# A two-layer diffusion step on one core: more of the merge in units of seven products, retention values centred beforehand, slot transposes reordered

## What is computed

```python
def _retention_output(o, g, gain):
    mu = jnp.mean(o, axis=-1, keepdims=True)
    var = jnp.mean(jnp.square(o - mu), axis=-1, keepdims=True)
    on = ((o - mu) * lax.rsqrt(var + EPS)).reshape(b, n, C_V).astype(g.dtype) * gain
    return jax.nn.silu(g) * on

def _merge(gates, a_o, b_o, c_o, w_pa, w_pb, w_pc, w_o):
    br = jnp.stack([a_o @ w_pa, b_o @ w_pb, c_o @ w_pc], axis=2)   # 3 x [tokens, 1024]
    merged = jnp.sum(jax.nn.sigmoid(gates) * br, axis=2)           # gates: 3 x [tokens, 1024]
    return merged @ w_o
```

## Time and profile before

| what | value |
|---|---|
| median of 3 runs | 1939.27 us (1939.24 to 1939.88) |
| profiled execution | 1939.07 us, of which its span is 1937.2 us |
| TensorE busy | 1818.0 us, 94% of the span |
| DVE, ACT, POOL busy | 638.3, 360.1, 210.0 us |
| moved by DMA | 553.10 MB, 286 GB/s over the span |
| mean granted TensorE clock | 0.999 of full speed |

### The profile page before, as it was taken

How to read it: one execution, slowest core, us unless ns; L and a number is a source line. 1 busy time by engine, 2 the same in 40 slices (tenths; PEclk the granted TensorE clock), 3 DMA queues, 4 the chain that set the end, 5 groups by cost and what they waited for, 6 DMA issues and landing times.

```text
span 1937.2 us, 21171 instructions
## 1 busy us (share of the span) xinstructions
PE 1818.0 (94%) x8802; PEld 1001.0 (52%) x8802; DVE 638.3 (33%) x1268; ACT 360.1 (19%) x835; POOL 210.0 (11%) x115
## 2 busy tenths in 40 slices
PE   6999999999999988788799999999999999888887
PEld 3565566799544433233365555669975343333323
DVE  2633347564211211111155333665532112111113
ACT  3223331111211110010132242221012010101002
POOL 0200003551100000000002000136400000000000
PEclk9999999999999999999999999999999999999999
DMA  9515151335799999999992244214456999999996
GB/s 391 200 72 223 66 224 69 131 131 205 302 396 427 427 428 427 427 428 428 413 381 98 87 180 174 98 44 174 174 228 275 428 426 428 428 427 428 427 428 273
DMA packets 54847, 553.10 MB, mean 286 GB/s; under 512 B 5985, under 2 KB 9953, under 8 KB 13281
## 3 DMA queue, kind: packets, MB, share of 16 engines
q1 hardware_dynamic: 50976, 549.13, 68.5%
q10 hardware_dynamic: 3776, 2.62, 0.4%
HBM read 547.54 MB, written 4.19 MB: 285 GB/s over the span
## 4 chain that ended last, share of the span: by engine, by line
PE 70%; DMA 29%; ACT 0%; DVE 0%; issue 0%; SPq 0%; DVEq 0%; ACTq 0%
PE psum L1423 14%; PE psum L1020 12%; PE psum L1234 11%; DMA ring<-in_w_up 8%; DMA dense<-in_w_down 8%; DMA ring<-in_w_gate 8%; PE psum L1022 6%; PE psum L1316 4%; PE psum L1148 4%; DMA dense<-in_w_gate 4%; PE psum L447 2%; PE psum L982 2%; PE psum L1226 2%; PE psum L1068 1%; PE psum L1393 1%; PE psum L1002 1%
## 5 line engine op out<-in xcount | busy, mean ns | idle before, releaser
L1423 PE MATMUL psum<-ring,dense 128*64 128x512 f32 x960 | 216.3, 595 | 31.9 <-DMA ring<-in_w_gate 18.0
L1020 PE MATMUL psum<-hT,ring 128*128 128x384 f32 x720 | 238.8, 488 | 0.0
L1020 PEld LDWEIGHTS psum<-hT,ring 128*128 128x128 f32 x720 | 135.0, 190 | 90.7 <-issue 1.4
L1423 PE MATMUL psum<-dense 128*64 128x512 f32 x704 | 158.7, 595 | 23.7 <-DMA dense<-in_w_gate 16.8
L1423 PEld LDWEIGHTS psum<-ring,dense 128*64 128x64 f32 x960 | 68.6, 137 | 170.7 <-issue 139.6
L2181 DVE TENSOR_TENSOR state<-state,psum 128x512 f32<-128x512 f32 x32 | 22.0, 687 | 372.3 <-PE psum L1423 334.2
L1022 PE MATMUL psum<-ring,hT 128*128 128x512 f32 x288 | 126.5, 594 | 0.0
L1423 PEld LDWEIGHTS psum<-dense 128*64 128x64 f32 x704 | 49.2, 137 | 129.1 <-issue 94.8
L2218 DVE COPY decays<-psum 16x512 f32<-16x512 f32 x60 | 41.3, 689 | 220.6 <-PE psum L1423 220.2
L1835 ACT ACTIVATE kcT<-psum 32x512 f32<-32x512 f32 x60 | 35.3, 588 | 423.6 <-PE psum L1423 423.2
L812 POOL TENSOR_TENSOR tmp<-square 128x384 f32<-128x384 f32 x5 | 5.0, 996 | 873.0 <-ACT square L1543 873.0
(11 more groups left out here) (285 smaller groups left out, 2401.5 us busy)
## 6 DMA issues: line engine op xcount, KB each, us to landing
dense<-in_w_gate SPq DMA_DIRECT2D x34, 2048.0 KB, 35.7
ring<-in_w_in SPq DMA_DIRECT2D x60, 1024.0 KB, 9.7
ring<-in_w_up SPq DMA_DIRECT2D x30, 2048.0 KB, 37.6
ring<-in_w_gate SPq DMA_DIRECT2D x30, 2048.0 KB, 36.1
wide<-in_w_up SPq DMA_DIRECT2D x22, 2048.0 KB, 37.6
dense<-in_w_down SPq DMA_DIRECT2D x20, 2048.0 KB, 40.3
ring<-in_w_mod SPq DMA_DIRECT2D x38, 1024.0 KB, 9.0
ring<-in_w_down SPq DMA_DIRECT2D x18, 2048.0 KB, 40.1
```

What stands on the lines that cost most here:

```text
L1020: last = M.matmul(psum[:, bank, 0:T], ring[:, n % RING, k, cols], hT[:, k, :], start=k == 0, stop=k == KD - 1)
L1423: last = M.matmul(psum[HALF * half:HALF * (half + 1), bank, :], lhsT(k), SPARE_BLOCKS[2 * kk + half] if spare else w[:, kk, half * SLAB:(h ...
```

## The change

1. The last four chunks of the first branch become two more units: `ALONE = 4` chunks alone, `PAIRS = 10` units (unit u uses branch (u + 2) // 4 and gate slab 10 + u // 2). POOL makes the sums for them: gate slab 10, the tokens of the first branch, half of its weights.
2. The buffers of the sums are placed anew. They now reach into the place of expert buffer 0 until the last unit, so SP loads expert 0's first half after the chain slabs, when all units are done; ring places come free at other counts.
3. The values and states of the retention are centred by DVE (`center`: a sum and a combination, four times a layer). `c_mean`, its wait and its correction go. ACT squares each head straight from the bank. `c_out(3)` and `c_var(2)` stand ahead of the units, `c_var(3)` inside the first.
4. In the first layer `mod` of the third chain slab goes ahead of the first `modT`; one `modT` goes behind the slot transposes, another behind the first gather. The rows of the third slab go to another buffer.

The diff, cut to its core:

```diff
@@ -61,7 +61,8 @@
-PAIRS = KD
+ALONE = 4
+PAIRS = (3 * KD - ALONE) // 2
@@ -238,12 +239,14 @@
-SUMS_X = [dense[:, 5648 + n * 1024:6672 + n * 1024] for n in range(3)]
-SUMS_Y = [dense[:, 4608:5632], decay_cols, dense[:, 10768:11792]]
-SUMS_Z = [dense[:, 9744:10768], dense[:, 11792:12816], dense[:, 12816:13840]]
-GATE_SUMS = {11: SUMS_X, 12: SUMS_Z, 13: SUMS_X, 14: SUMS_Z}
+SUMS_X = [dense[:, 4608 + n * 1024:5632 + n * 1024] for n in range(3)]
+SUMS_Z = [dense[:, a:a + 1024] for a in (7680, 10752, 11776)]
+SUMS_Y = [dense[:, a:a + 1024] for a in (8704, 9728, 12800)]
+GATE_SUMS = {10: SUMS_X, 11: SUMS_Z, 12: SUMS_X, 13: SUMS_Z, 14: SUMS_X}
+FIRST_BRANCH_SUMS = [in_chunks(x, 2) for x in (decay_cols[:, 512:1024], wide_cols[:, 6144:6656], wide_cols[:, 7680:8192])]
-Z_SUMS = {1: [in_chunks(x, 2) for x in (act[:, 0:T], flat(state1)[:, 0:T], rs[:])],
+Z_SUMS = {0: [in_chunks(x, 2) for x in (rs[:], merged[:, 5, :], merged[:, 7, :])],
+          1: [in_chunks(x, 2) for x in (act[:, 0:T], flat(state1)[:, 0:T], decay_cols[:, 0:T])],
@@ -377,17 +380,16 @@
-cmean_full = sem("cmean_full", 4)
-ccen = sem("ccen", 4)
+centered = sem("centered", 4)
-gate_full = sem("gate_full", KD)
-gate_exp = sem("gate_exp", KD)
-br_full = sem("br_full", KD)
-combined = sem("combined", 36)
+gate_full = sem("gate_full", ALONE)
+gate_exp = sem("gate_exp", ALONE)
+br_full = sem("br_full", ALONE)
+combined = sem("combined", 48)
@@ -496,7 +498,7 @@
-return steps + [("mod",) + m[2], ("modT",) + m[1], ("modT",) + m[2]]
+return steps[0:2] + [("mod",) + m[2], ("modT",) + m[0], ("modT",) + m[1], ("modT",) + m[2]]
@@ -516,13 +518,14 @@
-EARLY_CHAIN = [5, 4]
+EARLY_CHAIN = [4, 4]
-SECOND_SUMS = {("gate", 0): 7, ("gate", 2): 20, ("gate", 4): 28, ("branch", 4): 30, ("gate", 6): 34}
-THIRD_SUMS = {("gate", 0): 16, ("branch", 4): 31, ("gate", 6): 35}
-LAST_SUMS = {("branch", 4): 32, ("gate", 6): 36}
+SECOND_SUMS = {("gate", 0): 7, ("branch", 0): 14, ("gate", 2): 20, ("branch", 2): 28, ("gate", 4): 32, ("gate", 6): 40,
+               ("branch", 6): 42, ("gate", 8): 46}
+THIRD_SUMS = {("gate", 0): 15, ("branch", 0): 16, ("branch", 6): 43, ("gate", 8): 47}
+LAST_SUMS = {("branch", 6): 44, ("gate", 8): 48}
@@ -530,7 +533,7 @@
-return xgT[:, u * SLAB:(u + 1) * SLAB]
+return act if u == CHAIN_MODS - 1 else xgT[:, u * SLAB:(u + 1) * SLAB]
@@ -641,14 +644,12 @@
-elif kind == "w_in" and j < 11:
-    eng.wait_ge(gate_full, at(gate_full, 4 * (j - 8)))
+elif kind == "w_in" and j == 9:
+    eng.wait_ge(gate_full, at(gate_full, ALONE))
-    eng.wait_ge(pair_full["gate"], at(pair_full["gate"], 14 * (j - 10)))
-elif kind == "branch" and j == 0:
-    eng.wait_ge(br_full, at(br_full, KD))
+    eng.wait_ge(pair_full["gate"], at(pair_full["gate"], 14 * (j - 9)))
-    eng.wait_ge(pair_full["branch"], at(pair_full["branch"], 28 * j))
+    eng.wait_ge(pair_full["branch"], at(pair_full["branch"], 28 * j + 14))
@@ -716,9 +717,9 @@
-    if i == 0:
-        sp.wait_ge(pair_full["gate"], at(pair_full["gate"], 42))
-    if i == 1:
+    if i == 2:
+        sp.wait_ge(pair_full["branch"], at(pair_full["branch"], 14))
+    else:
         sp.wait_ge(pair_full["gate"], at(pair_full["gate"], 7 * PAIRS))
         sp.wait_ge(pair_full["branch"], at(pair_full["branch"], 7 * PAIRS))
 elif i == 4:
@@ -758,13 +759,12 @@
-buffer_free(0)
-load_expert(0)
 for c, (l, j) in enumerate(CHAIN[layer]):
     buffer_free(CHAIN_AT[c])
     sp.dma_start(whole_slab(BUFFERS[layer][CHAIN_AT[c]]), w_mod[l, j]).then_inc(chain_in[c], 16)
-buffer_free(1)
-load_expert(1)
+for i in range(2):
+    buffer_free(i)
+    load_expert(i)
 load_spare()
@@ -862,6 +862,9 @@
+if b == 0:
+    weight_sums(lambda kh, nh: branch_quarter(layer, 0, kh, nh)[:, :, 1, :], FIRST_BRANCH_SUMS)
+    return
@@ -882,29 +885,35 @@
-pool.wait_ge(att_full, at(att_full, HEADS_C))
+pool.wait_ge(ko_st, at(ko_st, 32))
+gate_sums(10)
+pool.wait_ge(a_done, at(a_done, HEADS_A))
+pool.wait_ge(o_read, at(o_read, 8))
+first_sums(lambda th, kh: z_quarter(0, th, kh), Z_SUMS[0])
 pool.wait_ge(qd_ready, at(qd_ready, 4))
-pool.wait_ge(ko_st, at(ko_st, 32))
+branch_sums(0)
+pool.wait_ge(gate_full, at(gate_full, ALONE))
+last_sum(h_quarter)
+pool.wait_ge(br_full, at(br_full, ALONE))
+last_sum(lambda th, kh: z_quarter(0, th, kh))
+pool.wait_ge(co_full, at(co_full, HEADS_C))
+pool.wait_ge(c_done, at(c_done, HEADS_C))
+pool.wait_ge(v_stored, at(v_stored, 32))
 gate_sums(11)
-pool.wait_ge(o_read, at(o_read, 8))
-pool.wait_ge(co_full, at(co_full, HEADS_C))
+pool.wait_ge(att_ready, at(att_ready, HEADS_C))
 first_sums(lambda th, kh: z_quarter(1, th, kh), Z_SUMS[1])
 last_sum(lambda th, kh: z_quarter(1, th, kh))
-pool.wait_ge(att_ready, at(att_ready, HEADS_C))
-pool.wait_ge(c_done, at(c_done, HEADS_C))
-pool.wait_ge(v_stored, at(v_stored, 32))
 branch_sums(1)
-pool.wait_ge(gate_full, at(gate_full, KD))
-last_sum(h_quarter)
+pool.wait_ge(pair_full["gate"], at(pair_full["gate"], 14))
 gate_sums(12)
-pool.wait_ge(br_full, at(br_full, KD))
+pool.wait_ge(pair_full["branch"], at(pair_full["branch"], 14))
 first_sums(lambda th, kh: z_quarter(2, th, kh), Z_SUMS[2])
 last_sum(lambda th, kh: z_quarter(2, th, kh))
-pool.wait_ge(pair_full["gate"], at(pair_full["gate"], 14))
+pool.wait_ge(pair_full["gate"], at(pair_full["gate"], 28))
 gate_sums(13)
-pool.wait_ge(pair_full["branch"], at(pair_full["branch"], 28))
+pool.wait_ge(pair_full["branch"], at(pair_full["branch"], 42))
 branch_sums(2)
-pool.wait_ge(pair_full["gate"], at(pair_full["gate"], 28))
+pool.wait_ge(pair_full["gate"], at(pair_full["gate"], 42))
 gate_sums(14)
@@ -986,7 +995,8 @@
-pe.wait_ge(z_read, max(f_of("mod", l, j) + 1, f - 1))
+same_bank = filler_bank(f) == filler_bank(f - 1)
+pe.wait_ge(z_read, max(f_of("mod", l, j) + 1, f if same_bank else f - 1))
@@ -1153,6 +1163,8 @@
+if kind == 2:
+    pe.wait_ge(centered, at(centered, 3))
@@ -1177,6 +1189,7 @@
+pe.wait_ge(centered, at(centered, 4))
@@ -1190,14 +1203,6 @@
-def c_mean(h):
-    if h == 0:
-        pe.wait_ge(st_ev, at(st_ev, 1))
-    pe.wait_ge(co_read, at(co_read, h + 1))
-    if h >= 1:
-        pe.wait_ge(ccen, at(ccen, h))
-    M.matmul(psum[:, TR[0], 0:T], ones, c_raw[:, h % 2, :], start=True, stop=True).then_inc(cmean_full, 1)
@@ -1206,15 +1211,12 @@
-for m in range(KD):
-    if m < HEADS_C:
-        c_att(m)
-    if 1 <= m <= HEADS_C:
+for m in range(ALONE):
+    c_att(m)
+    if m >= 1:
-    if 2 <= m <= HEADS_C + 1:
-        c_mean(m - 2)
-    if 3 <= m <= HEADS_C + 2:
-        c_var(m - 3)
+    if m >= 2:
+        c_var(m - 2)
@@ -1238,15 +1240,15 @@
-return lambda k: x[:, k, u % 4 // 2, u % 2 * P:(u % 2 + 1) * P]
+return lambda k: x[:, k, (u + 2) % 4 // 2, u % 2 * P:(u % 2 + 1) * P]
-branch = 1 + u // 4
+branch = (u + 2) // 4
-    j = 11 + u // 2
+    j = 10 + u // 2
@@ -1254,9 +1256,12 @@
-sums = [branch_weights(x.rearrange("p (k h n) -> p k h n", k=2, h=2), u) for x in SUMS_Y]
+if branch:
+    sums = [branch_weights(x.rearrange("p (k h n) -> p k h n", k=2, h=2), u) for x in SUMS_Y]
+else:
+    sums = [gate_weights(x, u) for x in FIRST_BRANCH_SUMS]
-if u % 4 == 0:
+if u % 4 == 2:
@@ -1266,6 +1271,8 @@
+if kind == "gate" and u == 0:
+    c_var(HEADS_C - 1)
@@ -1273,9 +1280,11 @@
-elif kind == "branch":
-    pe.wait_ge(gate_exp, at(gate_exp, KD))
-    pe.wait_ge(br_read, at(br_read, KD))
+elif kind == "gate":
+    pe.wait_ge(co_read, at(co_read, HEADS_C))
+else:
+    pe.wait_ge(gate_exp, at(gate_exp, ALONE))
+    pe.wait_ge(br_read, at(br_read, ALONE))
@@ -1285,6 +1294,8 @@
+c_out(HEADS_C - 1)
+c_var(HEADS_C - 2)
@@ -1372,7 +1383,7 @@
-fill(CHAIN_FILL[layer][EARLY_CHAIN[layer]:])
+fill(CHAIN_FILL[layer][EARLY_CHAIN[layer]:EARLY_CHAIN[layer] + 1])
@@ -1499,6 +1510,7 @@
+fill(CHAIN_FILL[layer][EARLY_CHAIN[layer] + 1:])
@@ -1730,33 +1742,35 @@
-for m in range(KD):
...
+def inverse_norm(h):
+    sc.wait_ge(cvar_full, at(cvar_full, h + 1))
...
+def head_read(h):
+    sc.wait_ge(co_full, at(co_full, h + 1))
+    if h >= 2:
+        sc.wait_ge(cvar_full, at(cvar_full, h - 1))
+    A_.activation(square[:, h % 2, :], psum[:, O[h % 2], 0:T], ACT.Square).then_inc(csq, 1)
+    if h >= 2:
+        sc.wait_ge(c_done, at(c_done, h - 1))
+    A_.activation(c_raw[:, h % 2, :], psum[:, O[h % 2], 0:T], ACT.Copy).then_inc(co_read, 1)
+for m in range(ALONE):
+    if m >= 2:
+        inverse_norm(m - 2)
+    if m >= 1:
+        head_read(m - 1)
-sc.wait_ge(gate_exp, at(gate_exp, KD))
-A_.preload_act_table(ACT.Sigmoid)
@@ -1764,8 +1778,14 @@
+head_read(HEADS_C - 1)
+inverse_norm(HEADS_C - 2)
 for u in range(PAIRS):
+    if u == 0:
+        inverse_norm(HEADS_C - 1)
+        sc.wait_ge(crs_read, at(crs_read, HEADS_C))
+        A_.preload_act_table(ACT.Sigmoid)
@@ -1793,7 +1813,7 @@
-read(CHAIN_FILL[layer][EARLY_CHAIN[layer]:])
+read(CHAIN_FILL[layer][EARLY_CHAIN[layer]:EARLY_CHAIN[layer] + 1])
@@ -1812,6 +1832,7 @@
+read(CHAIN_FILL[layer][EARLY_CHAIN[layer] + 1:])
@@ -1985,7 +2006,23 @@
+def center(n, x):
+    sums = decay_t[:].rearrange("p a h -> p (a h)")[:, 4 * n:4 * n + 4]
```

(63 more changed lines are left out.)

14 lines of the change are left out of this document (removed).

## The result

The changed kernel takes 1927.98 us (median of 4 runs, 1927.12 to 1928.27) against 1939.49 us of the kernel before on the same chip: ratio 0.994, 95% interval 0.9928 to 0.9953. The forecast was 1927.7 us. The profiled execution took 1928.27 us, with a span of 1926.4 us (1937.2 before).

What follows compares the result with a forecast made beforehand. TensorE's stream bounds each layer's first half, 2 MB weight transfers the experts, which start when TensorE lets them. Gains of 6.3 and 5.1 us from 1939.07 give 1927.7 us; own range 1925.5 to 1930, with rival 1 1925.3 to 1933.

Steps and rivals of the forecast that it cites:

- What bounds the kernel: Whole layer: TensorE paces the merge half, weight transfers the experts; the first replacement transfer moves with TensorE.
- Part 1: Merge: two more units, 27.32 us, replace four lone chunks, 30.96 us; gain 3.64 us a layer.
- rival 4: New units: weight load and matmul take turns, four units cost 20 us instead of saving 7.3; 1955 us, chance 1%.
- Part 2: Centring on DVE: four c_mean products go, 2.6 us a layer; TensorE waits 1.1 us at second-layer branch 1.
- Part 3: POOL's 15 sums for unit 0: done 8 us before TensorE needs the last; cost nothing.
- rival 3: Unit 0's third product: POOL's sums late, deciding from a factor of 1.35; 1949.7 us if doubled, chance 5%.
- Part 4: Queues: expert 0's load, 4.9 us, goes behind the last unit, covered by idle DMA time; cost nothing.
- Part 5: First layer's slot transposes: reached 0.8 us sooner, but one 0.65 us modT product precedes expert 0; net about 0.1 us.
- Rival 1: Merge: DVE falls further behind POOL, whose sums hold its steps past deadlines; 1933.5 us, chance 12%.

Runs made afterwards that it cites:

- the run with four more: The changed kernel with four more POOL sums of 1024 elements ahead of those for gate slab 10: 1928.66 us (one execution).

## Why the prediction was right

- **What bounds the kernel**: right. The merge is TensorE's stream, and the first replacement transfer moved with it, by 6.30 us in the first layer. The mean product put back costs its full length, and the centring alone wins its own.
- **Part 1**, 3.64 us a layer: measured 3.63. The narrow products show no loss; rival 4, where weight load and matmul take turns, is out.
- **Part 2**, 2.6 us a layer: measured 2.59 and 2.58. `center` was taken at 1.4 us and costs 1.32; in steps 8 to 10 DVE still has 0.39 us or more to spare. The wait in the second layer was named at the right place for the right reason, but at 1.1 us; it is 0.59 in this trace and costs 0.86. The step that was mis-sized is the start of POOL. I let POOL keep its distance from TensorE: its second token sum began 1245.63 - 1232.52 = 13.1 us behind `gate(0)`. A store releases it, and now the distance is 1240.86 - 1226.31 = 14.6 us. So L2095 waited out the second sum, not the third. In the kernel with the centring alone, where POOL starts nearly as before, DVE waits out the second and third sum as forecast and the wait is 0.94 us. The rest of the 1.1 is a reading: the prediction lets both DVE steps end 0.4 us behind a sum, but the earlier trace rows show 0.2 for L2059.
- **Part 3**: the count of POOL's work was right (23.97 against 23.8 us; 1.27 us for a sum of 512 elements where 1.3 was taken; 8.0 us early). The step that failed is where rival 3 decides. By POOL's own deadline that is not 8 us but 12.1, since the last token sum had 4.1 us of idle time ahead of it, so a factor of 1.5 on the sums and not 1.35: with 9.8 us more there is no wait for POOL. Yet these cost 1.7 us in the first layer, through DVE, a path that rival 3 left out, and past the deadline a wait costs more than itself, in the clock too.
- **Part 4**, nothing: right, shown by itself on the kernel before. The load for gate slab 12 and those behind it made no wait.
- **Part 5**, 0.1 us: measured 0.26. In the changed kernel TensorE does reach the slots sooner and waits 0.24 us for DVE there, as said; the `modT` work that moved behind the gather takes 0.53 us of the stream, not 0.65.

```profile
524.24 0.20 PE L1381 MATMUL psum<-const,tmp 16*128 16x16 f32 x1 [0.24 <-DVE tmp L2189]
...
530.90 0.61 PE L449 MATMUL psum<-const,state 128*128 128x128 f32 x4
531.43 4.94 PE L1434 MATMUL psum<-dense 128*64 128x512 f32 x22
```

The sum was 6.3 and 5.1 us; the stretches give 6.48 and 5.35. That the total is so near the forecast is partly luck: in the profiled execution the stretches won 0.4 us more than the sum, and 1.03 us that the sum doesn't have were lost outside them. The last stretch to the end of the span was 445.07 us before and is 445.16 to 445.83 in the kernels with ten units; why it differs was not tried. The forecast's own range, 1925.5 to 1930, doesn't come out of the bounds that it names: no wait and the whole 0.8 us of part 5 give 1925.8, and part 2's upper bound in both layers gives 1933.5.

Rival 1 is the one that lies nearest: DVE's steps are held for longer than forecast (2.72 and 2.39 us for L2089 and L2095 of chunk 1 in the second layer, against 0.56 and 0.36), but their multiplication still ends 0.7 us before branch 2 starts. It needs a few more sums to come true, as the run with four more shows.

## What to carry to other kernels

Where one engine's stream is full from end to end, price a change by what leaves and enters that stream, and compare executions over stretches between two named events: here the first layer's stretch repeats to 0.01 us where the totals scatter by 1 to 2. When work is moved onto GpSimd, don't stop at its own deadline: go through VectorE's steps that run beside it, give each one the length of the GpSimd sum that it can meet, and look for the first deadline that this passes. A step with a later reader (a head's own gate here) belongs behind the one that TensorE waits for.
